# Modulation of the first layer inside that layer's program, the late modulation rows between its projection steps

## What is computed

```python
def rms_norm(x, g):
    y = x32 * lax.rsqrt(jnp.mean(x32 * x32, axis=-1, keepdims=True) + EPS)
    return (y * g.astype(F32)).astype(x.dtype)

def adaln(cvec, w, b):
    e = jax.nn.silu(cvec) @ w + b
    return jnp.split(e, 3, axis=-1)

# for each of the two layers i
shift, scale, gate = adaln(c, mod_w[i], mod_b[i])
shift_c, scale_c, gate_c = adaln(c_ctx, mod_w[i], mod_b[i])
u_lat = rms_norm(h_lat, norm_g[i]) * (1.0 + scale[:, None, :]) + shift[:, None, :]
u_ctx = rms_norm(h_ctx, norm_g[i]) * (1.0 + scale_c) + shift_c
```

## Time and profile before

| | us |
|---|---|
| median of 3 runs | 3381.19 (3381.13 to 3385.32) |
| the profiled execution, whole | 3382.21 |
| its span, first to last instruction | 3380.4 |
| first product of the modulation | 10.61 |
| first transpose of the first norm | 117.42 |
| first product of the first layer's projection | 146.18 |

### The profile page before, as it was taken

The page is one execution under the profiler, slowest core; times in us unless marked ns, Lnnn a source line. Parts: engine busy times, 40 slices in busy tenths (PEclk is TensorE's granted clock), DMA queues, the critical chain, the costliest instruction groups (busy, mean ns, idle before and its releaser), DMA issues. The chain is left out here.

```text
span 3380.4 us, 35788 instructions
## 1 busy us (share of the span) xinstructions
PE 3155.4 (93%) x13406; PEld 1805.8 (53%) x13406; DVE 1364.7 (40%) x3204; ACT 818.3 (24%) x2252; POOL 485.4 (14%) x785
## 2 busy tenths in 40 slices
PE   8599999999999996999999999978999999678699
PEld 1245555555555543455555555536888886344374
DVE  0334544544644434133333334333555655242431
ACT  0103333333323320022332323211122221031131
POOL 0122321221321000212121111000011110010000
PEclk9699999999999997999999999997999999789899
DMA  8310101101004004120211103113120110222001
GB/s 299 101 50 26 50 25 39 37 25 50 25 28 147 1 3 133 52 73 26 75 50 50 51 33 127 47 43 93 26 51 26 26 51 1 66 77 78 25 1 50
DMA packets 135379, 189.09 MB, mean 56 GB/s; under 512 B 26356, under 2 KB 62356, under 8 KB 135204
## 3 DMA queue, kind: packets, MB, share of 16 engines
q1 hardware_dynamic: 135112, 186.72, 17.0%
q10 hardware_dynamic: 96, 0.10, 0.0%
HBM read 177.11 MB, written 9.68 MB: 55 GB/s over the span
## 5 line engine op out<-in xcount | busy, mean ns | idle before, releaser
L422 PE MATMUL a_psP<-a_w,a_uT 128*128 128x512 f32 x1536 | 696.6, 599 | 3.1 <-DVE a_uT L279 3.1
L1139 PE MATMUL b_psP<-b_w,b_uT 128*128 128x512 f32 x1024 | 461.6, 600 | 4.8 <-DMA b_w<-b_w_in 4.8
L422 PEld LDWEIGHTS a_psP<-a_w,a_uT 128*128 128x128 f32 x1536 | 280.4, 191 | 318.0 <-issue 314.4
L1139 PEld LDWEIGHTS b_psP<-b_w,b_uT 128*128 128x128 f32 x1024 | 188.4, 190 | 226.8 <-issue 226.8
L658 DVE TENSOR_REDUCE a_small<-a_psS 128x1 f32<-128x768 f32 (+1 forms) x192 | 140.8, 775 | 401.2 <-PE a_psS L450 401.2
L1831 PE MATMUL d_ps<-d_uT,d_w 128*128 128x264 f32 x1024 | 242.0, 390 | 13.9 <-DVE d_yT L2192 8.6
L1831 PEld LDWEIGHTS d_ps<-d_uT,d_w 128*128 128x128 f32 x1024 | 190.7, 191 | 48.8 <-DVE d_yT L2192 10.6
L1355 DVE TENSOR_REDUCE b_small<-b_psS 128x2 f32<-128x512 f32 x64 | 44.3, 692 | 411.4 <-PE b_psS L1191 411.4
L571 ACT ACTIVATE a_e<-a_psS,a_small 128x768 f32<-128x768 f32 (+1 forms) x192 | 144.0, 754 | 139.1 <-DVE a_small L658 138.6
L1284 ACT ACTIVATE b_e<-b_e,b_small 128x256 f32<-128x256 f32 x128 | 64.3, 503 | 320.1 <-DVE b_small L1369 320.1
L472 PEld LDWEIGHTS a_psO<-a_v,a_pT 128*128 128x128 f32 x896 | 115.1, 192 | 45.9 <-issue 45.9
(11 more groups left out here) (397 smaller groups left out, 4813.0 us busy)
## 6 DMA issues: line engine op xcount, KB each, us to landing
a_w<-a_w_in SPq DMA_DIRECT2D x16, 2048.0 KB, 8.2
b_w<-b_w_in SPq DMA_DIRECT2D x16, 2048.0 KB, 8.2
a_w<-mod_w SPq DMA_DIRECT2D x8, 2048.0 KB, 8.2
d_w<-a_w_in SPq DMA_DIRECT2D x32, 512.0 KB, 6.9
a_uT<-mod_w SPq DMA_DIRECT2D x4, 2048.0 KB, 8.5
b_bias<-bias_table SPq DMA_DIRECT2D x64, 128.0 KB
a_w<-a_w_out SPq DMA_DIRECT2D x2, 2048.0 KB, 7.8
b_w<-b_w_out SPq DMA_DIRECT2D x2, 2048.0 KB, 8.4
```

What stands on the lines that cost most here:

```text
L422: ins = nc.tensor.matmul(s.psP[:, x % 2, :], s.uT[:, a, t * P:(t + 1) * P], w[:, a, :], start=(a == 0), stop=(a == KD - 1))
L1139: ins = nc.tensor.matmul(s.psP[:, x % 4, :], lhsT, rhs, start=(a == 0), stop=(a == KD - 1))
```

## The change

`modulation` goes, and so does `Norm` in the first layer (the second layer keeps it). A new class `Opening` does both inside the first layer's program.

- First products: only shift and scale of the first layer (2048 columns, four banks) are computed ahead. `mod_w` comes in eight slices of 128 rows x 2048 columns (1 MB, rows of 8 KB), six slots in `yT`. For each slice there are four products, to partitions 0, 32 and 64 of one bank and 0 of a second. The four results get their bias on VectorE, are turned into columns by 16 small transposes on TensorE and put into `mod` by four VectorE instructions, without the way through device memory.
- All six tiles of x and ctx are loaded at once into homes of their own, x in 2 transfers a tile instead of 16, behind the first two weight slices. The six squares, the rstd and the multiplies run through for all tiles; tiles 0 and 1 are transposed ahead of the first products.
- Tiles 2 to 5 are transposed by TensorE behind steps 0 to 3; a tile is taken out of PSUM half by VectorE and half by ScalarE, one turn ahead of its use.
- Late products: the first layer's gate (2 banks) and the whole of the second layer's rows (6 banks) are multiplied behind steps 6 to 13, two slices a step: 8 gate slices (0.5 MB, two products each, partitions 0 and 32), then 8 slices of 1.5 MB with six products each, to partitions 0, 32 and 64 of two banks. Their weights take four slots in `yT` and are issued by SP between the loads of the projection weights. VectorE adds biases in turns 11, 15 and 16, SP stores the rows to `e_rows`; VectorE's first z step and the load of the gates wait for the stores, TensorE's first scores for the bias adds.
- The constants, the gain and all biases are issued on ScalarE's queue, 25 transfers, before its squares. The exponentials of lambda come behind the squares; VectorE waits for them before it multiplies the first tile.

```diff
...
+    FIRST = 4 * BANK
+    SLOTS, LATE_SLOTS = 6, 4
+    LATE_STEP = NT
...
+        self.place = [(0, 0), (0, 32), (0, 64), (1, 0)]
+        self.col_place = [s.psH[:, 0:KD], s.psO[:, 0:KD], s.psP[:, 0, 0:KD], s.psH[:, KD:2 * KD]]
+        self.late_place = [(0, 0, 0, 4), (0, 32, 0, 5)] + [(1 + c // 3, 32 * (c % 3), 1, c) for c in range(6)]
+
+    def late_after(self, x):
+
+        m = 2 * (x - self.LATE_STEP)
+        return range(m, m + 2) if 0 <= m < 2 * KD else range(0)
...
+    def sync(self, sp):
+        a = self.a
+        for r, src in enumerate((a["c"].rearrange("b d -> (b d)"), a["c_ctx"])):
+            sp.dma_start(self.cT[:, r * KD:(r + 1) * KD], src.rearrange("(p a) -> p a", a=KD)).then_inc(self.c_in, 16)
+        first = self.slices(a["mod_w"][0], slice(0, self.FIRST))
+        for m in range(2):
+            sp.dma_start(self.slots[m], first[m]).then_inc(self.m_in[m], 16)
+        for t, rows in enumerate(self.tiles):
+            k = P // len(rows)
+            for i, src in enumerate(rows):
+                sp.dma_start(self.h[t][i * k:(i + 1) * k, :], src).then_inc(self.h_in[t], 16)
+        for m in range(2, KD):
+            if m >= self.SLOTS:
+                sp.wait_ge(self.mm, m - self.SLOTS + 1)
+            sp.dma_start(self.slots[m % self.SLOTS], first[m]).then_inc(self.m_in[m % self.SLOTS], 16)
+
+    def late_sync(self, sp, m0, m1):
+        gate = self.slices(self.a["mod_w"][0], slice(self.FIRST, 3 * D))
+        rows = self.slices(self.a["mod_w"][1], slice(0, 3 * D))
+        for m in range(m0, m1):
+            if m < self.LATE_SLOTS:
+                sp.wait_ge(self.mm, KD)
+            else:
+                sp.wait_ge(self.late_mm, m - self.LATE_SLOTS + 1)
+            src = gate[m] if m < KD else rows[m - KD]
+            sp.dma_start(self.late[m % self.LATE_SLOTS][:, 0:src.shape[1]], src).then_inc(self.late_in[m % self.LATE_SLOTS], 16)
...
+    def tensor(self, pe):
+        nc, s = self.nc, self.s
+        c = self.act_c.rearrange("p (r a) -> p r a", r=2)
+        for t in range(2):
+            self.transpose(pe, t)
+        pe.wait_ge(self.c_silu, 1)
+        for m in range(KD):
+            pe.wait_ge(self.m_in[m % self.SLOTS], 16 * (m // self.SLOTS + 1))
+            for j, (b, p0) in enumerate(self.place):
+                ins = nc.tensor.matmul(s.psP[p0:p0 + 2, b, :], c[:, :, m], self.slots[m % self.SLOTS][:, j * BANK:(j + 1) * BANK],
+                                       start=(m == 0), stop=(m == KD - 1))
+            ins.then_inc(self.mm, 1)
+        for j, (b, p0) in enumerate(self.place):
+            pe.wait_ge(self.er_done, j + 1)
+            for i in range(4):
+                ins = nc.tensor.transpose(self.col_place[j][:, 2 * i:2 * i + 2],
+                                          self.er[p0:p0 + 2, b, i * P:(i + 1) * P], s.ident[p0:p0 + 2, p0:p0 + 2])
+        ins.then_inc(self.cols, 1)
...
+    def tensor_before(self, pe, x):
+        if x < NT:
+            pe.wait_ge(self.dve_done, x + 1)
+            pe.wait_ge(self.act_done, x + 1)
+
+    def tensor_after(self, pe, x):
+        nc, s = self.nc, self.s
+        c = self.act_c.rearrange("p (r a) -> p r a", r=2)
+        if x + 2 < NT:
+            self.transpose(pe, x + 2)
+        for m in self.late_after(x):
+            if m == 0:
+                pe.wait_ge(self.dve_done, NT)
+                pe.wait_ge(self.act_done, NT)
+            pe.wait_ge(self.late_in[m % self.LATE_SLOTS], 16 * (m // self.LATE_SLOTS + 1))
+            w = self.late[m % self.LATE_SLOTS]
+            for b, p0, layer, j in self.late_place:
+                if layer == m // KD:
+                    j -= 4 * (1 - layer)
+                    ins = nc.tensor.matmul(s.psS[p0:p0 + 2, b, :], c[:, :, m % KD], w[:, j * BANK:(j + 1) * BANK],
+                                           start=(m % KD == 0), stop=(m % KD == KD - 1))
+            ins.then_inc(self.late_mm, 1)
...
+    def scalar(self, act):
+        nc = self.nc
+        for t in range(NT):
+            act.wait_ge(self.h_in[t], 16 * len(self.tiles[t]))
+            if t:
+                act.wait_ge(self.sq, t)
+            nc.scalar.activation(self.dump, self.h[t], ACT.Square, scale=D ** -0.5, accum_out=self.ss[:, t:t + 1]).then_inc(self.sq, 1)
...
+    def vector(self, dve):
+        nc, s = self.nc, self.s
+        for t in range(NT):
+            self.norm(dve, t)
+        dve.wait_ge(self.b_in, 16 * len(self.place))
+        dve.wait_ge(self.mm, KD)
+        for b, p0 in self.place:
+            nc.vector.tensor_tensor(self.er[p0:p0 + 2, b, :], s.psP[p0:p0 + 2, b, :], self.br[p0:p0 + 2, b, :], ALU.add
+                                    ).then_inc(self.er_done, 1)
+        dve.wait_ge(self.gain_in, 16)
+        dve.wait_ge(self.cols, 1)
+        for j in range(4):
+            half = slice(4 * (j % 2), 4 * (j % 2) + 4)
+            cols = self.col_place[j].rearrange("p (a r) -> p r a", r=2)
+            if j < 2:
+                ins = nc.vector.tensor_copy(s.mod[:, :, 1, half], cols)
+            else:
+                ins = nc.vector.scalar_tensor_tensor(s.mod[:, :, 0, half], cols, 1.0,
+                                                     self.g[:, half].unsqueeze(1).to_broadcast([P, 2, 4]), ALU.add, ALU.mult)
+            ins.then_inc(self.mod_set, 1)
...
+        places = {last - 3: (0, 2), last + 1: (2, 5), last + 2: (5, 8)}.get(x, (0, 0))
+        for i in range(*places):
...
+            if 1 <= b <= 3:
+                self.opening.late_sync(sp, (0, 4, 14)[b - 1], (4, 14, 16)[b - 1])
+            if b == 3:
+                self.opening.late_store(sp)
...
+        sp.wait_ge(self.opening.late_stored, 16 * len(self.opening.late_place))
...
+        opening = self.opening
+        opening.tensor(pe)
         for i, x, y in self.turns():
+            if i == 0:
+                pe.wait_ge(opening.late_rows, len(opening.late_place))
             if i is not None:
                 scores(i)
             if x is not None:
+                opening.tensor_before(pe, x)
...
+                opening.tensor_after(pe, x)
...
+        for t in range(2):
+            opening.scalar_evacuate(act, t)
         for i, x, y in self.turns():
+            if x and x + 1 < NT:
+                opening.scalar_evacuate(act, x + 1)
...
+                if x == self.LEAD:
+                    dve.wait_ge(self.opening.late_stored, 16 * len(self.opening.late_place))
...
+        for t in range(2):
+            opening.vector_evacuate(dve, t)
         for i, x, y in self.turns():
+            if x and x + 1 < NT:
+                opening.vector_evacuate(dve, x + 1)
+            if i is None:
+                opening.late_vector(dve, x)
...
-            sp.dma_start(s.ident[:, :], a["ident"]).then_inc(const_in, 16)
-            for row in range(4):
-                src = a["rope_cos"] if row % 2 == 0 else a["rope_sin"]
-                sp.dma_start(s.tab[:, row, :, :], src.rearrange("(t p) d -> p t d", p=P)).then_inc(const_in, 16)
-            for i, name in enumerate(("a_qn_g", "a_kn_g")):
-                sp.dma_start(s.gains[:, 0, i * DH:(i + 1) * DH], a[name][0].partition_broadcast(P)).then_inc(const_in, 16)
-            sp.dma_start(s.gains[:, 1, :], a["a_subln_g"][0].partition_broadcast(P)).then_inc(const_in, 16)
-            for r in range(4):
-                sp.dma_start(raw[:, r, :], a["a_lam"][0, r].partition_broadcast(P)).then_inc(const_in, 16)
-            norm.sync(sp)
+            opening.sync(sp)
             mixer.sync(sp)
 
         @block.vector
...
+            nc.vector.memset(s.half[:, :], -0.5).then_inc(half_set, 1)
+            nc.vector.memset(s.eps[:, :], EPS).then_inc(half_set, 1)
+            opening.silu(dve)
...
-            norm.vector(dve)
+            opening.vector(dve)
...
+            opening.tanh(act)
+            act.dma_start(s.ident[:, :], a["ident"]).then_inc(const_in, 16)
+            for row in range(4):
+                src = a["rope_cos"] if row % 2 == 0 else a["rope_sin"]
+                act.dma_start(s.tab[:, row, :, :], src.rearrange("(t p) d -> p t d", p=P)).then_inc(const_in, 16)
+            for i, name in enumerate(("a_qn_g", "a_kn_g")):
+                act.dma_start(s.gains[:, 0, i * DH:(i + 1) * DH], a[name][0].partition_broadcast(P)).then_inc(const_in, 16)
+            act.dma_start(s.gains[:, 1, :], a["a_subln_g"][0].partition_broadcast(P)).then_inc(const_in, 16)
+            for r in range(4):
+                act.dma_start(raw[:, r, :], a["a_lam"][0, r].partition_broadcast(P)).then_inc(const_in, 16)
+            opening.biases(act)
+            opening.scalar(act)
             act.wait_ge(lam_done, 1)
             nc.scalar.activation(lexp, lsum, ACT.Exp).then_inc(lam_exp, 1)
-            norm.scalar(act)
...
-            modulation(nc, first_sem, s, a["c"], a["c_ctx"], a["mod_w"], a["mod_b"], e_rows)
-            if upto >= 1:
-                diff_layer(nc, first_sem, s, a, e_rows[0], h1)
```

(26 more changed lines are left out.)

183 lines of the change are left out of this document (101 added, 82 removed).

## The result

The changed kernel takes **3352.4 us** (3349.2 to 3354.4, four runs) against 3381.2 us for the kernel before (3380.1 to 3385.3, four runs): a ratio of 0.9912, interval 0.9895 to 0.9929. It is faster by 29 us. The forecast was 60 us, and its range ended at 3345. The profiled execution has a span of 3349.4 us and took 3351.2.

A forecast was written before the change was run, and what follows sets the result against it. TensorE, full from the projection's start, was taken as the bound: projection at 59.2 us plus 26.5 added gives 85.7 against 146.2, 60.5 us less, so 3320.7 us, range 3306 to 3345.

The forecast's parts named there:

- What bounds the kernel: First layer: TensorE is full from the projection's start at 146.18 us; moving that start moves the end by as much.
- The price of a product: Modulation products on different partitions overlap: a first slice 1.72 us, a gate slice 0.86, a second-layer slice 1.72.
- rival 1: Modulation products: the narrow products don't overlap, 48 us more, 3369 us; serial products given a chance of 0.13.
- When the products can start: Program start, before TensorE's first transpose: bounds of 25 and 45 us, the middle taken, 35 us.
- late end: Program start: constants share engines with bulk and end last at 36 us, ScalarE stalled in issues: first transpose at 45 us.
- Rival 2: Program start: constants gate everything, x on half the engines, first transpose at 60 us, 25 us more, 3346; chance 0.05.
- The sum up to the projection: From first transpose at 35.0 us through two tiles, eight slices and the tail: projection starts at 59.2 instead of 146.18.
- tail: Between the eight slices and the projection: bias adds, small transposes, VectorE steps, half a tile modulated and hops, 6.6 us.
- What is added behind it: Behind the projection's start: transposes 3.5 us, short step 0.8, late products 20.6, switches 1.6; sum 26.5.
- the switches: Projection steps with late products: changing between narrow and full products eight times, 0.2 us each, 1.6 us.
- Weights for the late products: Steps 10 to 13: 3 MB wanted in 10.3 us, 291 GB/s, under 309: no cost; 12 us more without that cover.
- The e rows and the biases: Behind the projection's start: e row stores have about 14 us, bias adds in VectorE's turns some 0.3: both counted as nothing.

The follow-up runs named there:

- e1: Changed kernel with SP waiting for the twelve constants before it issues the first weight slice and the x tiles: 3333.0 us.
- e9: Changed kernel with a slice's four first products on partitions 0, 32, 64 and 96 of one bank: 3346.0 us.
- e5: Changed kernel with SP waiting for the constants and each x tile read as 128 consecutive rows in one transfer: 3321.2 us.
- e3: Changed kernel with each x tile read as 128 consecutive rows in one transfer, constants left where they were: 3336.1 us.
- e2: Changed kernel with the twelve constants issued by SP ahead of the bulk instead of by ScalarE, no wait added: 3334.6 us.
- e6: e2 with x tiles 0 and 1 loaded before the weight slices, tiles 2 to 5 and their squares and norms later, exponentials first: 3323.4 us.
- e8: Changed kernel with the second layer's six products of a slice on positions 0 and 32 of three banks: 3358.2 us.
- e12: e6 with the projection's first weights issued ahead of tiles 2 to 5: 3317.3 us.
- e10: e1 with x's eight runs of eight rows at a pitch of 9 rows instead of 64: 3335.9 us.
- e11: e1 with x read as sixteen runs of four rows instead of eight runs of eight: 3329.1 us.

## Why the prediction was wrong, step by step

**What bounds the kernel: right.** Each us at the projection's start is one at the first score product: the later start and the 2.7 us more behind it (29.2, not 26.5) make up the whole miss there.

**The price of a product: right.** Eight first slices took 14.70 us for the 13.76 of the sum (13.90 in e1); two gate slices 1.89 (1.72), two of the second layer's 3.61 (3.44). That is 64 records in 14.70 us, where 0.43 each would be 27.5, and 24 in 3.61 for 10.3. So rival 1 is out: three positions give a factor of 2.86, and four in e9 one of 3.5 (3.44 / 0.98). The 2.38 for three of the Trainium skill ("TensorE: Matmul & The Clock Gate", Part 3), which I had cited against the forecast, doesn't fit these records: the measurement decides.

**When the products can start: this step failed.** It put the first transpose at 35 us between 25 and 45; it came at 59.0. Three things in it were wrong.
- The late end let ScalarE stall for as long as constants and bulk together last, and reckoned all bulk at 386 GB/s. x came at 114 GB/s (e1), for one part because its transfers have an outermost dimension of 8, for another for a reason that is open. In the earlier trace rows x was bound by the issue of 64 pieces in 22.98 us, so no row showed its rate with large pieces; I took that of weights as if it held for any shape. Worth 13.4 us (e1 to e5, of which sixteen runs give 8.6) to 15.5 (change to e3).
- The stall itself was named, as part of the late end, and then priced at the middle. It is worth 13.7 us (e3 to e5) to 15.7 (change to e1). What the Trainium skill says of it ("DMA: Bandwidth & Descriptors", Queues, rings and completion order: queues taken in turns, packet by packet) pointed to the late end. In e1 and e2 the constants have no bulk beside them on another queue, and both start 16 us earlier. They show that the two queues at once are the cause, though not that this rule is how.
- Rival 2 was this outcome: the constants gate everything and x comes on half the engines, first transpose at 60. Against the profiled execution it gave 3346.7, and that took 3351.2: 1.0 less at the start, 0.3 less in the sum up to the projection, 2.7 more behind it and 3.1 more behind the first score product. The range itself went up to a start at 59 us, which is where it came, so it was also too short behind that start, by these 2.7 and 3.1; the rest of the 7 us beyond its end is the spread of executions. I gave rival 2 a chance of 0.05, on the ground that 9 MB take 23 us and that nothing more is issued then. That was the same 386 GB/s again: one unproven rate carried both the forecast and the case against its rival. (Its "few hundred small packets per engine" for each constant is too many: ScalarE's queue carried 5364 packets up to 50 us for all 25 transfers, 335 an engine.)

**The sum up to the projection: right,** 23.9 us for 24.2 (14.70 of slices, 5.6 from their end to the projection's start for a tail of 6.6, and 3.6 of transposes).

**What is added behind it: 29.2 for 26.5.** The late products and their neighbours went as reckoned (steps 6 to 13, 78.7 us to 55.9 before, 22.8; the sum had 22.2 with the switches). The steps before took 51.3 us to 45.4 before, 5.9 for 4.3. There the first step takes 9.72 us for 16 records, at a mean granted clock of 0.73 in its stretch, where one at the higher clock takes 7.03; I had left that start as it was, with 1.9 us for it. TensorE had been nearly idle for 5.6 us, from 77.3 to 82.87. And two waits for VectorE's rotation cost 1.1 (0.45 and 0.65), for 0.8. Behind step 13 another 0.5 went (29.8 us for 29.3), 0.28 of it in a third such wait. Weights for the late products: no wait in the trace, right. The e rows and the biases: nothing, right.

The starts of steps 6 and 14 before, and of step 14 after (step 6 is at 134.14 above):

```profile
191.56 7.03 PE L422 MATMUL a_psP<-a_w,a_uT 128*128 128x512 f32 x16
...
247.44 7.03 PE L422 MATMUL a_psP<-a_w,a_uT 128*128 128x512 f32 x16
```

```profile
212.86 7.03 PE L571 MATMUL a_psP<-a_w,a_uT 128*128 128x512 f32 x16
```

**The later layer.** In the delta-rule layer the same work takes 130.0 us (2328.7 to 2458.7) at a mean granted clock of 0.95, and took 127.2 before (2362.9 to 2490.1) at 0.97. From the first score product to the end, ten of the thirteen changed kernels take 2.4 to 6.4 us more than the kernel before, e6 and e8 0.6 and 0.3 less, and e12 2.4 less. Each of these is one execution, and executions of one kernel lie up to 9.4 us apart (e10, whose profiled one is its slowest; e12's is its fastest). Whether the change costs something there, and what sets it, is open.

## What to carry to other kernels

When loads move from a quiet queue into the start of a program, ask of each transfer how many parts its outermost dimension has and what goes on beside it on the other queue; a rate measured for one shape need not hold for another (x came at 114 GB/s in eight runs and 244 in sixteen, where the core moved over 400 once a tile was one run). Small loads belong ahead of the bulk, and not beside it on the queue of an engine whose first computation everything waits for: on the bulk's own queue (e2) or on another with the bulk held back (e1) they cost the same here, 3334.6 and 3333.0 us. Then order loads and small computations by who needs them first: moving the constants gave 18 us here (e2), and ordering the rest another 17 (e12).

## What the runs showed of the hardware

- A DMA issue on ScalarE's queue took 0.4 to 0.8 us, and 9.5, 14.4 and 13.5 us when bulk came on SP's queue and three of the constants were already out. With the constants alone (e1) the same issues took 0.57 to 0.67.
- 0.5 MB of x in two transfers of 64 partitions, issued by SP, took 4.6 to 5.4 us with eight outermost runs (e1, e10, e2) and 2.1 us with sixteen (e11). The whole core moved 205 to 244 GB/s in the changed kernel and in e1 while such x came, 247 in e11, with the engines shown as busy, and up to 425 in e5, where a tile is one run in one transfer.
- Two-wide products of 512 columns on the output partitions 0, 32, 64 and 96 run side by side almost wholly: 0.98 us for a slice of four, where one product takes 0.86. Their order within a slice didn't matter with two to a position (3.61 and 3.62 us), and cost a round with three (6.18 where 5.2 is the least).
